# Turning ten of twelve expert blocks with VectorE into PSUM, in cycles of three rounds

## The reference

```python
q = (xt @ wq)                       # 8 heads x 256
s1, s2 = halves of q times subkeys1, subkeys2
v1, i1 = top_k(s1, 16); v2, i2 = top_k(s2, 16)
vals, pos = top_k(v1[:, None] + v2[None, :], 16)
ids = e1 * 128 + e2                 # 16 experts per head and token
g = softmax(vals)
a = einsum('td,thkd->thk', xt, u_tab[ids])
hid = gelu(a) * g
y = einsum('thk,thkd->td', hid, v_tab[ids])
x = layer_norm(alpha * x1 + y)
```

## Time and profile before

| | us |
|---|---|
| Median of 3 runs | 1054.47 (1052.27 to 1055.65) |
| Profiled execution, its own time | 1055.02 |
| Its span | 1053.2 |
| PE, DVE, ACT, POOL busy | 1030.0, 841.3, 456.0, 452.2 |

### The profile page before, as it was taken

One profiled execution on the slowest core, in us unless ns is written; L12 is line 12 of the kernel. 1 busy time (PEld: TensorE's weight loads), 2 busy tenths in 40 slices (PEclk: granted clock), 3 DMA queues, 4 the chain that ended last, 5 costly groups with the idle time before them and its releaser, 6 DMA issues.

```text
span 1053.2 us, 20477 instructions
## 1 busy us (share of the span) xinstructions
PE 1030.0 (98%) x6739; PEld 925.1 (88%) x6739; DVE 841.3 (80%) x1579; ACT 456.0 (43%) x658; POOL 452.2 (43%) x332
## 2 busy tenths in 40 slices
PE   8999999999999999999999999997999999999996
PEld 8978898999999999999999999734888888888885
DVE  4475457877999999988888888415999999999887
ACT  4474434544443434444444444202444444454442
POOL 3920000058888888888888888872000000000000
PEclk9999999999999999999999999998999999999999
DMA  9777589645665668877877777798888888888782
GB/s 320 251 272 254 187 286 294 219 120 108 140 139 139 138 138 182 177 174 168 176 166 173 164 173 163 157 320 272 272 270 267 271 264 270 266 270 269 242 244 94
DMA packets 155284, 223.07 MB, mean 212 GB/s; under 512 B 48624, under 2 KB 101168, under 8 KB 155248
## 3 DMA queue, kind: packets, MB, share of 16 engines
q1 hardware_dynamic: 117808, 221.17, 66.0%
q0 software_dynamic: 37440, 1.43, 10.1%
HBM read 204.59 MB, written 17.96 MB: 211 GB/s over the span
## 4 chain that ended last, share of the span: by engine, by line
PE 47%; POOL 39%; issue 8%; DVE 3%; DMA 2%; ACT 1%; SPq 0%; POOLq 0%; DVEq 0%; ACTq 0%
POOL expert_weights L523 39%; PE ps L1495 29%; PE ps L1398 15%; DMA expert_weights<-gw,cell 1%; PE ps L1285 1%; PE ps L1263 1%; DVE w_lo L1017 1%; ACT w_hi L653 1%; DVE small L774 1%; DMA xres<-in_x_dram 0%; DMA v_raw<-in_peer_v_dram 0%; PE ps L1273 0%; PE ps L1238 0%; DVE v_lo L1123 0%; DVE xres L1179 0%
## 5 line engine op out<-in xcount | busy, mean ns | idle before, releaser
L523 POOL DMA_INDIRECT expert_weights<-gw,cell x256 | 412.3, 1611 | 246.0 <-DVE gw L999 162.7
L1439 PE MATMUL ps<-act_hi,uT_hi 128*128 128x256 f32 x1024 | 295.0, 288 | 0.0
L1439 PE MATMUL ps<-act_hi,uT_lo 128*128 128x256 f32 x1024 | 289.9, 283 | 0.0
L1439 PE MATMUL ps<-act_lo,uT_hi 128*128 128x256 f32 x1024 | 289.6, 283 | 0.0
L739 ACT ACTIVATE v_hi<-v_raw 128x512 fp32r<-128x512 f32 x256 | 147.7, 624 | 211.0 <-PE ps L1495 161.0
L1439 PEld LDWEIGHTS ps<-act_hi,uT_hi 128*128 128x128 f32 x1024 | 196.6, 192 | 0.2 <-issue 0.2
L1439 PEld LDWEIGHTS ps<-act_lo,uT_hi 128*128 128x128 f32 x1024 | 196.6, 192 | 0.0
L1439 PEld LDWEIGHTS ps<-act_hi,uT_lo 128*128 128x128 f32 x1024 | 196.3, 192 | 0.0
L1123 DVE TENSOR_TENSOR v_lo<-v_raw,v_hi 128x512 fp32r<-128x512 f32 x256 | 165.1, 687 | 17.0 <-ACT v_hi L739 16.9
L1495 PE MATMUL ps<-v_hi,hid_hi 128*128 128x512 f32 x464 | 144.8, 392 | 5.8 <-DVE hid_lo L1140 5.8
L1085 DVE STREAM_TRANSPOSE uT_raw<-u_raw 128x1024 f32<-128x1024 f32 x63 | 136.1, 2161 | 13.9 <-PE ps L1439 13.5
(11 more groups left out here) (175 smaller groups left out, 1438.3 us busy)
## 6 DMA issues: line engine op xcount, KB each, us to landing
v_raw<-in_peer_v_dram SPq DMA_DIRECT2D x152, 512.0 KB, 4.5
u_raw<-in_peer_u_dram SPq DMA_DIRECT2D x65, 512.0 KB
u_raw<-in_peer_u_dram SPq DMA_DIRECT2D x252, 128.0 KB, 2.8
expert_weights<-zeros SPq DMA_DIRECT2D x16, 1024.0 KB, 12.2
w_raw<-in_w_in_dram SPq DMA_DIRECT2D x7, 2048.0 KB, 9.3
g_in<-expert_weights SPq DMA_DIRECT2D x104, 128.0 KB, 3.6
w_raw<-in_peer_wq_dram SPq DMA_DIRECT2D x4, 2048.0 KB, 10.8
w_raw<-in_w_out_dram SPq DMA_DIRECT2D x2, 2048.0 KB, 10.0
```

What stands on the lines that cost most here:

```text
L523: pool.indirect_dma_start(out=table_cells, out_offset=bass.IndirectOffsetOnAxis(ap=cell[:, t, k:k + 1], axis=0), in_=gw[:, t, k:k + 1], in ...
L1439: ins = pe.matmul(ps[:, bank, 0:T], (uT_hi, uT_hi, uT_lo)[part][:, slot, k, :], (act_hi, act_lo, act_hi)[part][:, k, :], start=(k == 0 and ...
```

## The change

Three rounds now make a cycle, and there are seven cycles. In a cycle ten of the twelve blocks are turned by DVE: slots 1 to 3 of every round, and slot 0 of the third one. PE turns slot 0 of the first two. DVE's transpose writes two PSUM banks in place of `uT_raw`, which is gone: bank pairs 2-3 and 0-1 in turn for slots 1 to 3, 6-7 for slot 0. ACT rounds from these banks, and DVE's rest of such a block is `rest_uT`, with the banks as one operand. Since the banks 0 and 1 are needed from the first turn on, the last four of the 44 blocks put their products into banks 4 and 5. `turn` no longer waits for PE's product (`a_done`) but for DVE's own rest of an earlier block (`uT_lo_done`), and before the first one for ACT's gelu of block 39. SP's waits and the kind of load for slot 0 follow.

```diff
+CYCLE = 3
+CYCLES = ROUNDS // CYCLE
+TURNS = (3, 3, 4)
+TURNED = (0, 3, 7)
...
-    uT_raw = sb("uT_raw", [P, 4, KD, P], 185 * K1)
...
+    def turned_into(r, slot):
+        return 6 if slot == 0 else (2, 0)[(r + slot + 1) % 2]
...
+        def next_round(j, r):                                   # SP
+            b = CYCLE * GROUP * j + block_of(NPRE + GROUP * (r + 1))
+            if r < 2:
+                sp.wait_ge(s["u_read"], 2 * j + (NPRE + r + 1))
+            else:
+                sp.wait_ge(s["u_turned"], sum(TURNS) * j + TURNED[2])
+            (load_u_squares if r == 1 else load_u)(b, 0)
             for k in range(1, GROUP):
-                sp.wait_ge(s["u_turned"], (GROUP - 1) * i + k)
-                load_u_squares(GROUP * i + block_of(NPRE + GROUP + k), k)
+                sp.wait_ge(s["u_turned"], sum(TURNS) * j + (TURNED[r] + k))
+                load_u_squares(b + k, k)
...
-        def round_turned(turned, slot):                         # ACT
+        def round_turned(turned, banks, slot):
             act.wait_ge(s["u_turned"], turned)
             act.activation(uT_hi[:, slot].rearrange("p a b -> p (a b)"),
-                           uT_raw[:, slot].rearrange("p a b -> p (a b)"), ACT.Copy)...
+                           ps[:, banks:banks + 2, :].rearrange("p a b -> p (a b)"),
+                           ACT.Copy).then_inc(s["uT_hi_done"], 1)
...
-            gelu(n, n % 2, block_of(n))
+            gelu(n, (4 if n >= NPRE - 4 else 0) + n % 2, block_of(n))
...
-        def turn(n, slot, landed):                              # DVE
+        def turn(n, r, slot, landed):
+            banks = turned_into(r, slot)
             dve.wait_ge(s[f"u_in{slot}"], landed)
-            dve.wait_ge(s["a_done"], n - 3)
-            dve.transpose(uT_raw[:, slot].rearrange("p k (c i) -> p c k i", c=NQ),
+            dve.wait_ge(s["uT_lo_done"], n - (1 if slot == 3 or (r, slot) == (0, 1) else 3 if slot == 0 else 2))
+            dve.transpose(free(ps[:, banks, :], (Q, NQ), (P, KD), (1, Q)),
                           u_raw[:, slot, :].rearrange("p (c j k) -> p c k j", c=NQ, k=KD)).then_inc(...)
-        def rest_turned(n, slot): ...
+        dve.wait_ge(s["act_done"], NPRE - 4)
+        with dve.Fori(0, CYCLES) as j:
+            for r in range(CYCLE):
+                n = CYCLE * GROUP * j + (NPRE + GROUP * r)
+                for k in range(1, GROUP):
+                    ...
+                    turn(n + k, r, k, ...)
+                    if k == 1 and r < 2:
+                        rest_uT(n, 6, 0)
+                    else:
+                        rest_uT(n + (k - 1), turned_into(r, k - 1), k - 1)
+                if r == 1:
+                    turn(n + GROUP, 2, 0, ...)
+                rest_uT(n + (GROUP - 1), turned_into(r, GROUP - 1), GROUP - 1)
...
-                expert_inputs(k, k % 2)                         # PE, first 44 blocks
+                expert_inputs(k, (4 if last else 0) + k % 2)
...
-                if k == 1 and not last:                         # PE, rounds
-                    transpose_u(16 * i + (8 * NPRE + 32), 0, 6)
+                if k == 1 and r != 1 and not last:
+                    landed = 2 * 16 if r == 0 else (2 + NQ) * 16 + 16
+                    transpose_u((2 + NQ) * 16 * j + (8 * NPRE + landed), 0, 6)
```

More of the change, by code:

```diff
@@ L396, in _ @@
             load_u_squares(block_of(NPRE + k), k)
[L397 to L402 removed]
+        def next_round(j, r):
[5 more added lines that the diff above has]
+            (load_u_squares if r == 1 else load_u)(b, 0)
+            for k in range(1, GROUP):
+                sp.wait_ge(s["u_turned"], sum(TURNS) * j + (TURNED[r] + k))
+                load_u_squares(b + k, k)
+        with sp.Fori(0, CYCLES - 1) as j:
+            for r in range(CYCLE):
+                next_round(j, r)
+        for r in range(CYCLE - 1):
+            next_round(CYCLES - 1, r)
         sp.wait_ge(s["scattered0"], 16 * SLOTS)
[L405 removed]
+        sp.wait_ge(s["u_turned"], sum(TURNS) * (CYCLES - 1) + TURNED[2])
         load_fill(0)
         for k in range(1, GROUP):
[L408 removed]
+            sp.wait_ge(s["u_turned"], sum(TURNS) * (CYCLES - 1) + TURNED[2] + k)
             load_fill(k)
@@ L718, in _, with main_step @@
             else:
-                round_turned(1, 1)
-            gelu(n, n % 2, block_of(n))
-        def main_step(i, k, tail):
+                round_turned(1, turned_into(0, 1), 1)
+            gelu(n, (4 if n >= NPRE - 4 else 0) + n % 2, block_of(n))
+        def main_step(j, r, k, tail):
+            turned = sum(TURNS) * j + TURNED[r]
             if k < 2:
-                round_turned((GROUP - 1) * i + (k + 2), k + 2)
+                round_turned(turned + (k + 2), turned_into(r, k + 2), k + 2)
             elif not tail:
-                if k == 2:
-                    round_uT(i + (NPRE + 1), 6, uT_hi[:, 0])
-                else:
[L730 to L733, removed]
+                if k == 3:
+                    round_turned(sum(TURNS) * j + (sum(TURNS) + 1 if r == 2 else TURNED[r + 1] + 1),
+                                 turned_into((r + 1) % CYCLE, 1), 1)
+                elif r == 1:
+                    round_turned(sum(TURNS) * j + TURNED[2], turned_into(r, 0), 0)
+                else:
+                    round_uT(2 * j + (NPRE + (r + 2) // 2), 6, uT_hi[:, 0])
+            n = GROUP * r + NPRE + k
+            gelu(CYCLE * GROUP * j + n, 4 + k % 2, CYCLE * GROUP * j + block_of(n))
         def round_v(m, k, landed):
@@ L742, in _ @@
         act.wait_ge(s["route_done"], len(BATCHES))
-        with act.Fori(0, ROUNDS - 1) as i:
+        with act.Fori(0, CYCLES - 1) as j:
+            for r in range(CYCLE):
+                for k in range(GROUP):
+                    main_step(j, r, k, False)
+        for r in range(CYCLE):
             for k in range(GROUP):
-                main_step(i, k, False)
-        for k in range(GROUP):
-            main_step(ROUNDS - 1, k, True)
+                main_step(CYCLES - 1, r, k, r == CYCLE - 1)
         for k in range(BODY):
@@ L1467, in main_four @@
                 expert_inputs(k, 4 + k % 2)
-                if k == 1 and not last:
-                    transpose_u(16 * i + (8 * NPRE + 32), 0, 6)
-        with pe.Fori(0, ROUNDS - 1) as i:
-            main_four(i, False)
-        main_four(ROUNDS - 1, True)
+                if k == 1 and r != 1 and not last:
+                    landed = 2 * 16 if r == 0 else (2 + NQ) * 16 + 16
+                    transpose_u((2 + NQ) * 16 * j + (8 * NPRE + landed), 0, 6)
+        with pe.Fori(0, CYCLES - 1) as j:
+            for r in range(CYCLE):
+                main_four(j, r, False)
+        for r in range(CYCLE):
+            main_four(CYCLES - 1, r, r == CYCLE - 1)
         def fill(i, opens=False):
```

25 lines of the change are left out of this document (6 added, 19 removed).

## The result

| | before | after |
|---|---|---|
| Median (range) of the shared runs | 1054.35 (1052.27 to 1055.65, 4 runs) | 1046.83 (1046.11 to 1047.53, 4 runs) |
| Profiled execution, its own time | 1055.02 | 1046.11 |
| Its span | 1053.2 | 1044.3 |

The ratio is 0.9932 with an interval of 0.992 to 0.9943. The change makes the kernel 7.5 us faster; 7.4 was forecast.

The account below looks back on a forecast made before the run. Bound: the later of scatters (724.85) and PE's stage (724.05). Less 10.35 and 6.3 us, outputs start at 717.75 and block 1 comes 7.4 earlier: 1054.47 - 7.4 = 1047.1 us, range 1043.5 to 1050 (1055.5 with no-change cases).

Parts of the forecast that it names:

- The later of two paths: Start of the outputs: the later of scatters (724.85) and PE's stage (724.05); moving one alone gains at most 0.8 us.
- X: PE in the rounds: seven fewer blocks turned by PE, 0.90 us each, save 6.3 us if PE stays the bound.
- the lead of a rest's end over its product: DVE in the rounds: 3.7 us at best; seven turned blocks in a row take 2.1, leaving over 1 us.
- The reading of block 1: Output block 1: its V can go out by 712.7, allowing 720.4, so it doesn't hold the start at 723.25.
- The price of writing PSUM: DVE's transposes in the rounds: writing PSUM leaves them at 2161 ns, 2.08 us start to start.
- rival A: Ten transposes a cycle: slower into PSUM, DVE becomes the bound; 1067 us at 2.5 us each, about 1116 at 3.2; chance 0.14.
- B: Rounds: transposes take 2.25 to 2.35 us, PE's saving is near 0, no change, 1053 us; chance 0.07.
- DVE's spare: DVE in the rounds: 1.5 us left per cycle of 36.36 us, or 0.15 us per transpose.
- S: Scatters in the rounds: removing rests with two SBUF operands frees 10.35 us of holds; scatters land at 710.8 instead of 721.2.
- rival C: Scatters: the holds come from something else and stay, so outputs start no earlier, no change, 1054.5 us; chance 0.09.
- SP's wait for the last scatter: Sign ahead of the outputs: SP's wait falls from 5.6 us to 1 or 2 if the forecast is right.
- C's doubled hold: Scatters: if transposes into PSUM hold them, about twice the time under hold, landing 10 us later, 1064 us.

Follow-up runs that it names:

- e1: Changed kernel with PE turning slot 0 of every round again; DVE's other nine turns a cycle still go into PSUM: 1052.83 us.
- e2: Changed kernel with ten of twelve blocks still turned by DVE, but into an SBUF buffer, so their rests have two SBUF operands: 1063.27 us.
- e9: Changed kernel with scatters delayed by two GpSimd fillings of an unused tile at each of 14 places, from the 104th scatter on: 1055.08 us.
- e12: Changed kernel plus 24 unread PE transposes of the identity after the last fill, DVE's order kept: 1046.78 us.
- e11: Changed kernel with DVE making block 0's `hid` right after its `v_lo`, plus 24 unread PE transposes after the last fill: 1045.43 us.
- e4: Changed kernel plus one DVE reduction over 128x512 with one SBUF input at the end of each round: 1048.03 us.
- e5: Changed kernel plus one DVE addition over 128x512 with two SBUF inputs at the end of each round: 1049.0 us.
- e6: Changed kernel with DVE turning all twelve blocks of a cycle, PE only the very first block: 1061.33 us.
- e3: Changed kernel with scatters delayed by one GpSimd filling of an unused tile at each of 14 places: 1048.29 us.
- e8: Changed kernel with SP loading weights ahead of block 1's V and DVE making block 0's `hid` right after its `v_lo`: 1049.77 us.
- e10: Changed kernel with only DVE's order changed, block 0's `hid` right after its `v_lo`: 1046.29 us, one run of 2598.04 us left out of the ratio.

## Why the prediction was right

**The later of two paths.** This was the step that carried the forecast. e1 moved the scatters by 12.6 us and gained 1.4. e2 shortened PE's rounds by 6.4, held the scatters longer, and lost 9. e9 had the short rounds and late scatters and gained nothing. The change has both and gains 7.5. The start of the outputs is a maximum, and the profile of before showed both its arguments 0.8 us apart.

**X.** From the first expert product to the first fill it takes 418.38 us after and 424.95 before: 6.57 us, forecast 6.3. The cycle is the 36.36 us of the sum, and within it the lead of a rest's end over its product falls from 3.80 us to 1.63, where the prediction took off 2.1. The start of the outputs came at 717.71 on before's clock (forecast 717.75), and block 1 at 722.99 (forecast 723.25), since block 0 took 5.28 us at the low clock where 5.5 were taken. Block 1 is thus 7.7 us earlier.

That the start fits to 0.04 us is luck. PE's last fill was forecast at 713.56 and ended at 714.10 on before's clock: the rounds saved 0.27 more, but the fills took 45.92 us where before they took 45.11. PE's idle time after it was 3.61 us where 4.2 were taken. The three differences cancel. e12, whose program is the same up to the last fill, took 44.16 us for them, so this stage alone differs by over a microsecond from one execution to another.

The reading of block 1 was wrong in one point. The V transfer that the prediction calls block 1's (issued at 722.99 before) is block 2's: SP loads the weights between V of blocks 1 and 2, and block 1 hangs on it only because DVE makes `v_lo` of block 2 before `hid` of block 1. It was to go out by 712.7 and allow block 1 at 720.4. It went out at 714.58, 715.57 on before's clock, and `hid` of block 1 was done at 722.33, 0.7 us before PE was free for it at 722.99. It didn't hold, but nearly. In e11, where block 0 takes 2.86 us, the chain of transfers behind the last scatter ends in block 2's wait.

The profiled executions lie 8.9 apart; 1.0 of that is the earlier start of the whole frame, and the medians lie 7.5 apart.

**The price of writing PSUM.** 2141 ns against 2161: the nearest rows gave the right value, and rivals A and B fell with it. The rest from PSUM takes 1218 ns against 1199, nine times a cycle 0.2 us. The Trainium skill, "VectorE: DVE Perf Modes", section on the TRN2 errata, would have given an estimate of 65 ns each; the traces show 3 ns (before, both forms in one run) and 19 (after against before), and in e2 the rests from SBUF took 1211 ns and those from PSUM 1204.

**DVE's spare, somewhat too small.** The prediction left 1.5 us a cycle; e4 shows about 1.9. The 0.4 us is the transpose, which took 2.04 us start to start where 2.08 was taken. What the twelve rests and the waits leave for ten transposes came out as in the sum, 36.36 - 14.0, so the 2.23 us at which rival A starts stands. But it is not made up as the sum had it: in e4 the 0.8 us of waiting for ACT are gone, and a rest costs 1.13 us start to start ahead of a transpose and 1.19 ahead of another rest, not 1.10.

**S, right in the hold and wrong in the landing.** The holds vanished to the last one: 10.35 us of excess before, and no scatter of the rounds over 1.58 us after or in e1. e4 and e5 show the mechanism without the change around it. An addition of 128x512 with both inputs in SBUF made the 0.33 us of excess in e5's scatter above, so rival C falls. The Trainium skill, "SBUF — State Buffer", section "Who interferes with whom", has a second statement, that `tensor_tensor` did not stall transfers that GpSimd issues; for these indirect transfers the runs show the contrary. But the landing was forecast 10.3 us earlier and came 7.7 earlier. The last scatter starts only 9.0 earlier, for two gaps between scatters that the profile calls "issue" lasted 1.88 and 1.98 us where before they lasted 1.62 and 0.66. (In e1 it starts 12.6 us earlier, since GpSimd also waits once for earlier scatters to land, and this wait took 1.72 us there, 4.28 before and 3.96 after.) And it takes 6.4 us to land instead of 5.1. So the scatters' path would have allowed the start at about 713.45 + 3.65 = 717.1 (landing on before's clock, and from landing to product as in the earlier trace rows), not at 714.5. PE's stage was the later path by 0.6 us, as far as this estimate goes, and not by 3.2: the margin that the prediction claimed wasn't there. SP's wait for the last scatter shows it too: 3.1 us, where 1 or 2 were forecast. With another microsecond of gaps or landing the scatters would have been the bound, and the gain smaller.

**The rivals' other side.** A's picture is e6's. "The scatters stay late" is e9's, at 1055.08; C had 1054.5. C's doubled hold, priced at 1064, has its likeness in e2 at 1063.27: there the excess did double, though not through transposes into PSUM. What should have been said of the step is that time under hold doesn't scale with the number of windows, since the two loops can fall into step.

Left open: what the two gaps of almost 2 us between scatters are; whether e11 is faster than the change. Not tried: taking the hold away that `w_lo` (L1041) puts on the first scatters, from 221 to 236.

## What to carry to other kernels

Where a stage waits for two things, work out the time of both before pricing an edit: here each half of the change alone gave 1.4 us or a loss, and the two together 7.5. Look at what an engine's operand placement does to an engine that it never talks to; the timeline of both side by side, at the starts of the long ones, shows it. And price the landing of a transfer with its neighbours at the new time, not with its old latency.

## What was not expected of the hardware

- A GpSimd indirect scatter that starts inside a VectorE operation with two SBUF inputs lasts until 1.42 us after that operation's end (all 21 long ones of the rounds before; e5's pad of 0.68 us does it too, 15 of 15, to 1.45 us). It isn't held by a transpose, a reduction, or a subtraction with one input in PSUM.
- The last scatter takes 3.0 us to land when no V transfer is under way (e2, e9; 2.9 in e3, where they are just ending) and 6.4 beside them (after).
- A VectorE transpose of 128x1024 fp32 costs the same into PSUM (2141 ns) as into SBUF (2161).
- Block 0 ran at a granted clock of 0.50, the lower level, after PE had idled 3.61 us (after) and 4.95 (before), and at 1.00, the upper one, after 2.47 us (e8), after filler transposes (e11), and after these and 1.76 us (e12). Between the two, e10 shows a mean of 0.65 over 717.33 to 722.00 after 4.08 us of idle time, and e1, after 4.11 us, products at the upper level first and a mean of 0.65 over 724.76 to 727.50. Of idle times alone these rows make no sharp border.
